# State-space groups of a two-block kernel: a new order of VectorE's and ScalarE's steps, and three VectorE helpers computed head by head

## The reference

```python
def ssd_chunked(x, dt, a, bm, cm, h0, need_y):
    xc = (x * dt[..., None]).reshape(b, nc, SSD_CHUNK, g, r, p)
    cs = jnp.cumsum((dt * a).reshape(b, nc, SSD_CHUNK, g, r), axis=2)
    decay_to_end = jnp.exp(cs[:, :, -1:] - cs)
    chunk_states = jnp.einsum('bclgn,bclgr,bclgrp->bcgrpn', bc, decay_to_end, xc)
    chunk_decay = jnp.exp(cs[:, :, -1])
    def step(hc, inp):
        st, dec = inp
        return hc * dec[..., None, None] + st, hc
    h_last, h_in = lax.scan(step, h0, (chunk_states, chunk_decay))
    lmat = jnp.exp(jnp.where(lower, seg, -jnp.inf))
    cb = jnp.einsum('bclgn,bcsgn->bclsg', cc, bc)
    y = (jnp.einsum('bclsg,bclsgr,bcsgrp->bclgrp', cb, lmat, xc)
         + jnp.einsum('bclgn,bcgrpn,bclgr->bclgrp', cc, h_in, jnp.exp(cs)))
```

## Time and profile before

| | before |
|---|---|
| median of 3 runs | 2844.2 us |
| lowest and highest | 2837.63 and 2851.76 us |
| the profiled execution: its own time | 2849.4 us |
| its span in the trace | 2847.4 us |
| PE busy | 2603.6 us, 91% |
| VectorE busy | 1271.1 us, 45% |
| GpSimd busy | 1637.9 us, 58% |
| ScalarE busy | 913.4 us, 32% |
| mean granted TensorE clock | 0.958 |

### The profile page before, as it was taken

The page is one execution under the profiler, slowest core; times in us unless marked ns, Lnnn a source line. Parts: engine busy times, 40 slices in busy tenths (PEclk is TensorE's granted clock), DMA queues, the critical chain, the costliest instruction groups (busy, mean ns, idle before and its releaser), DMA issues.

```text
span 2847.4 us, 38601 instructions
## 1 busy us (share of the span) xinstructions
PE 2603.6 (91%) x15451; PEld 2224.3 (78%) x15451; DVE 1271.1 (45%) x2224; ACT 913.4 (32%) x1607; POOL 1637.9 (58%) x1414
## 2 busy tenths in 40 slices
PE   6989998999998989989998999989989898879998
PEld 5679987875787777778877788778777777779998
DVE  1545502327646677775123112122454878743311
ACT  2245533115422322224113102042353333243542
POOL 1007775750366666654784788754225676657785
PEclk9999999999899999999999999999989999989999
DMA  6456553237432111112422333332533222245554
GB/s 175 139 166 184 145 133 108 89 122 233 132 98 66 50 47 52 51 38 71 159 89 74 89 102 90 89 104 89 168 124 108 74 63 82 60 126 163 163 155 126
DMA packets 425807, 312.92 MB, mean 110 GB/s; under 512 B 12561, under 2 KB 423219, under 8 KB 424627
## 3 DMA queue, kind: packets, MB, share of 16 engines
q1 hardware_dynamic: 421744, 297.36, 35.4%
q10 hardware_dynamic: 3330, 12.98, 1.2%
q0 software_dynamic: 576, 0.43, 0.2%
HBM read 303.40 MB, written 7.34 MB: 109 GB/s over the span
## 4 chain that ended last, share of the span: by engine, by line
PE 66%; DVE 18%; POOL 7%; issue 5%; ACT 2%; DMA 1%; ACTq 0%; POOLq 0%; DVEq 0%; SPq 0%
PE PS L695 34%; POOL rounded L2506 7%; PE PS L1032 7%; DVE mid_a L2254 5%; PE PS L753 5%; PE PS L718 3%; DVE mid_v L2306 2%; PE PS L1039 2%; PE PS L1159 2%; PE PS L638 2%; PE PS L1081 1%; PE PS L1072 1%; DVE mid_v L2327 1%; PE PS L950 1%; PE PS L962 1%
## 5 line engine op out<-in xcount | busy, mean ns | idle before, releaser
L2506 POOL TENSOR_TENSOR rounded<-ring,rounded 128x512 fp32r<-128x512 f32 (+1 forms) x872 | 1128.3, 1326 | 727.1 <-ACT rounded L1294 487.6
L695 PE MATMUL PS<-rounded 128*128 128x256 f32 (+1 forms) x6864 | 1154.5, 330 | 29.2 <-DVE rounded L2443 8.1
L695 PEld LDWEIGHTS PS<-rounded 128*128 128x128 f32 x6864 | 1026.0, 192 | 154.3 <-issue 23.6
L2529 POOL TENSOR_TENSOR rounded<-ring,constants 128x512 fp32r<-128x512 f32 x216 | 227.4, 1083 | 291.1 <-PE PS L695 148.5
L1032 PE MATMUL PS<-rounded 128*128 128x512 f32 (+1 forms) x1536 | 356.8, 390 | 8.0 <-POOLq L2476 4.4
L1032 PEld LDWEIGHTS PS<-rounded 128*128 128x128 f32 x1536 | 279.7, 191 | 71.1 <-issue 9.1
L1294 ACT ACTIVATE rounded<-ring 128x2048 fp32r<-128x2048 f32 (+1 forms) x99 | 179.8, 1822 | 164.3 <-DMA ring<-in_w_mlp_dram 57.2
L2254 DVE SCALAR_TENSOR_TENSOR mid_a<-PS,V,mid_a 128x510 f32<-128x510 f32 (+3 forms) x256 | 182.0, 713 | 78.2 <-ACT mid_a L1600 71.1
L1039 PE MATMUL PS<-rounded 128*128 128x256 f32 x1152 | 167.8, 309 | 0.0
L1039 PEld LDWEIGHTS PS<-rounded 128*128 128x128 f32 x1152 | 159.6, 213 | 5.9 <-issue 2.4
L2416 DVE SCALAR_TENSOR_TENSOR xT<-PS,mod,xT 128x256 f32<-128x256 f32 x40 | 17.9, 481 | 264.7 <-PE PS L695 264.7
(11 more groups left out here) (244 smaller groups left out, 3288.2 us busy)
## 6 DMA issues: line engine op xcount, KB each, us to landing
ring<-in_w_mlp_dram SPq DMA_DIRECT2D x64, 1024.0 KB, 5.6
ring<-in_w_in_dram SPq DMA_DIRECT2D x56, 1024.0 KB, 5.3
ring<-in_ada_w_dram SPq DMA_DIRECT2D x48, 1024.0 KB, 5.2
ring<-in_w_in_dram SPq DMA_DIRECT2D x81, 512.0 KB, 4.0
ring<-in_w_up_dram SPq DMA_DIRECT2D x44, 512.0 KB, 5.2
ring<-in_w_ssd_o_dram SPq DMA_DIRECT2D x16, 1024.0 KB, 5.7
ring<-in_w_out_dram SPq DMA_DIRECT2D x12, 1024.0 KB, 5.0
ring<-in_w_down_dram SPq DMA_DIRECT2D x16, 704.0 KB, 4.9
```

Of the source, the lines that this page charges most:

```text
L695: mm = pe.matmul(PS[:, b, 0:cols], w[:, k, m * P:(m + 1) * P], x(half * kt + k), start=(half == 0 and k == 0 and n_pass == 0), stop=(half ...
L2506: ins = pool.tensor_tensor(lo[:, r], raw[:, r], hi[:, r], ALU.subtract)
L2529: ins = pool.tensor_tensor(hi[:, r], raw[:, r], ones[:, 0:1].broadcast_to([P, 512]), ALU.mult)
```

## The change

Four things are edited.

1. The order of VectorE's turn: `masks` goes ahead of `taps(0)`; `weights(1)` goes from behind `outputs(0)` to ahead of `starts`; in layer 0 `silu(3)` goes ahead of `outputs(2)`.
2. The order of ScalarE's turn: `tanh_of(0)` goes behind `decays(0)` and `decays(1)`; in layer 0 `tanh_of(2)` goes ahead of the `middle` of tile 3.
3. `weights`, `starts` and `outputs` no longer do one multiplication over all four heads and then one addition. They do one `scalar_tensor_tensor` for each head that does both, with the head's factor as a per-partition scalar. In `weights` that is 4 instructions of 128x128 in place of 2 of 128x512; in each of the two rounds of `starts`, 8 of 128x64 in place of 4 of 128x256; in `outputs`, for each direction, 4 of 128x64 in place of 2 of 128x256. The waits inside (`settle`) that stood between multiplication and addition go.
4. TensorE waits for 8 counts of `hin_ready` in place of 1, since each of the last 8 instructions of `starts` now gives one.

```diff
--- before.py
+++ after.py
@@ -1086,7 +1086,7 @@
 
                     pe.wait_ge(*c.need(m_ready))
                     if t == 0:
-                        pe.wait_ge(*c.need(hin_ready))
+                        pe.wait_ge(*c.need(hin_ready, 2 * GH))
                     else:
                         pe.wait_ge(*c.need(y_done))
                     for r in range(GH):
@@ -1134,7 +1134,7 @@
                 turn_of(0, first=True)
                 counted = [(tile_ready, 4 + nz), (dve_freed, 4 + nz), (chan_ready, 4), (tok_turned, 3),
                            (cb_ready, 1), (seg_in, 2 * ny), (cb_masked, 1), (seg_ready, ny), (tok_ready, 3),
-                           (xw_ready, 6), (st_ready, 1), (m_ready, ny), (hin_ready, 1), (y_done, ny),
+                           (xw_ready, 6), (st_ready, 1), (m_ready, ny), (hin_ready, 2 * GH), (y_done, ny),
                            (y_ready, ny), (split_ready, 4)]
                 counted += [(slot_loaded[(s0 + q) % SLOTS], 32 if q == 2 else 16) for q in range(4)]
                 with c.loop(GROUPS // 2 - 2, [(q, 2 * k) for q, k in counted]):
@@ -1660,9 +1660,9 @@
 
                     after = g + 1 < GROUPS
                     to_tok(first)
-                    tanh_of(1 - p, 0)
                     decays(0)
                     decays(1)
+                    tanh_of(1 - p, 0)
                     if not first:
                         squares_of(last)
                     middle(g, 1 - p, 1)
@@ -1676,10 +1676,12 @@
                     tanh_of(1 - p, 1)
                     if ny > 2:
                         decays(2)
-                    middle(g, 1 - p, 3)
-                    tanh_of(1 - p, 2)
-                    if ny > 2:
+                        tanh_of(1 - p, 2)
+                        middle(g, 1 - p, 3)
                         decays(3)
+                    else:
+                        middle(g, 1 - p, 3)
+                        tanh_of(1 - p, 2)
                     tanh_of(1 - p, 3)
                     if after:
                         round_of_group(g + 1, 2)
@@ -2285,11 +2287,11 @@
 
                 def weights(g, t):
 
-                    lo = dt_lo[:, :, :]
-                    step(dve.tensor_tensor(lo, bc_mid(cb_lo[:, t, :], GH), heads_of(dt, t, 0, g, P), ALU.mult))
                     dve.wait_ge(*c.need(dtu_ready))
-                    settle()
-                    step(dve.tensor_tensor(per_head(dt_up[:, t % 2, :]), lo, per_head(dt_up[:, t % 2, :]), ALU.add))
+                    for r in range(GH):
+                        m = dt_up[:, t % 2, r * P:(r + 1) * P]
+                        step(dve.scalar_tensor_tensor(out=m, in0=cb_lo[:, t, :], scalar=dt[:, t, g * GH + r:g * GH + r + 1], in1=m,
+                                                      op0=ALU.mult, op1=ALU.add))
                     dve.wait_ge(*c.need(e_ready))
                     settle()
                     dve.tensor_tensor(ex[:, t % 2, :], dt_up[:, t % 2, :], PS[:, 7 - t % 2, :], ALU.mult).then_inc(*c.made(m_ready))
@@ -2303,16 +2305,15 @@
                     for n in range(1, 3):
                         settle()
                         for d, order in enumerate((F_STATES, B_STATES)):
-                            step(dve.tensor_tensor(per_head(hin[:, 3 * d + n, :]), per_head(hin[:, 3 * d + n - 1, :]),
-                                                   heads_of(edec, order[n], 128 + 32 * d, g), ALU.mult))
-                        settle()
-                        for d in range(2):
-                            h = hin[:, 3 * d + n, :]
-                            ins = dve.tensor_tensor(h, h, st[3 * d + n], ALU.add)
-                            if n == 2 and d == 1:
-                                ins.then_inc(*c.made(hin_ready))
-                            else:
-                                step(ins)
+                            for r in range(GH):
+                                e, m = 128 + 32 * d + g * GH + r, slice(r * HD, (r + 1) * HD)
+                                ins = dve.scalar_tensor_tensor(out=hin[:, 3 * d + n, m], in0=hin[:, 3 * d + n - 1, m],
+                                                               scalar=edec[:, order[n], e:e + 1], in1=st[3 * d + n][:, m],
+                                                               op0=ALU.mult, op1=ALU.add)
+                                if n == 2:
+                                    ins.then_inc(*c.made(hin_ready))
+                                else:
+                                    step(ins)
 
                 def outputs(g, p, t):
 
@@ -2321,11 +2322,13 @@
                     step(dve.tensor_tensor(ys, PS[:, 3 + t % 2, 0:GW], xd[:, t % 2, :], ALU.add))
                     for d, hs in enumerate((HF, HB)):
                         if t in hs:
-                            step(dve.tensor_tensor(per_head(yi), per_head(PS[:, 5, d * GW:(d + 1) * GW]),
-                                                   heads_of(edec, t, 32 + 64 * d, g), ALU.mult))
                             settle()
-                            step(dve.tensor_tensor(ys, ys, yi, ALU.add))
-                            settle()
+                            for r in range(GH):
+                                e, m = 32 + 64 * d + g * GH + r, slice(r * HD, (r + 1) * HD)
+                                step(dve.scalar_tensor_tensor(out=ys[:, m], in0=PS[:, 5, d * GW + r * HD:d * GW + (r + 1) * HD],
+                                                              scalar=edec[:, t, e:e + 1], in1=ys[:, m],
+                                                              op0=ALU.mult, op1=ALU.add))
+                    settle()
                     dve.scalar_tensor_tensor(out=yg[:, t, bass.ds(g * GW, GW)], in0=ys, scalar=0.5, in1=sz[p][:, t, :],
                                              op0=ALU.mult, op1=ALU.mult).then_inc(*c.made(y_done))
                     settle(y_done)
@@ -2333,17 +2336,17 @@
                 def turn_of(g, p, products=True):
 
                     nxt = g + 1
+                    masks()
                     if products:
                         taps(nxt, 1 - p, 0)
-                    masks()
                     weights(g, 0)
                     if products:
                         silu(1 - p, 0)
+                    weights(g, 1)
                     starts(g)
                     if products:
                         taps(nxt, 1 - p, 1)
                     outputs(g, p, 0)
-                    weights(g, 1)
                     if products:
                         silu(1 - p, 1)
                         taps(nxt, 1 - p, 2)
@@ -2355,9 +2358,10 @@
                         if products:
                             taps(nxt, 1 - p, 3)
                         weights(g, 3)
+                        if products:
+                            silu(1 - p, 3)
                         outputs(g, p, 2)
                         if products:
-                            silu(1 - p, 3)
                             gate_of_z(1 - p, 0)
                         outputs(g, p, 3)
                         if products:
```

## The result

The kernel after runs in 2765.24 us, the median of 4 runs (2760.26 to 2768.98). The kernel before, measured beside it, has 2847.98 us, also over 4 runs (2837.63 to 2852.98). The ratio is 0.9713, with a 95% interval of 0.9679 to 0.9747: faster by 2.9%, against a forecast of 2763 us.

A forecast was written before the change was run, and what follows sets the result against it. TensorE was taken to bound the kernel, held up by a late VectorE. Layer 0's 25 us, layer 1's 47 and its last turn's 9 make 81 us off 2849.4, giving 2768, or 2763 us as median; range 2728 to 2802.

The forecast's parts named there:

- What bounds the kernel: Whole kernel: TensorE, busy 91%; time can be won only where it waits, for a late VectorE, or runs slowly.
- Masks first: Head of each turn: PE's waits for the masks, 1.3 and 1.2 us, go; the delay of `taps(0)` stays hidden.
- Narrow instructions: By-head VectorE instructions: 0.20 us for 64 columns, 0.27 for 128; upper ends 0.28 and 0.35 us.
- the rival of dear narrow instructions: All three helpers: no overlap, 0.28 and 0.35 us per instruction, so 53 us gained, 2791 us; chance 20%.
- `starts`: VectorE ahead of chunk 0: from 6.7 to 4.2 us, since the fused form reads PSUM and runs beside GpSimd.
- Layer 1: Its turns with products: 44.1 us loses 5.0 of waits and 1.7 of slow clock, to 37.4; 47 us over seven.
- the rival "slower": Both layers: `weights` ahead of `starts` holds up TensorE, about 6 us late in layer 1; 2870 us; chance 5%.
- the forecast's own signs of being wrong: `starts` stretched beside GpSimd, a wait for `starts` in layer 1, or a mean layer 0 turn of 61 us or more.
- Layer 0: Its turns: waits 6.6 to 3.1 us (2.1 before chunk 0, 1.0 before chunk 3), slow clock stays; 25 us over seven.
- The clock never falls in layer 0: Rival: the clock holds behind the new 2.1 us wait; 3.3 us more per turn, 23 us, 2740 us; chance 20%.
- The last turn of layer 1: Turn without products: 4.1 us wait goes, of 5.2 some 1.3 stay, about 1 us slow clock goes; 9 us.

The follow-up runs named there:

- the experiment: Kernel after with `masks` put back behind `taps(0)`, nothing else: 2774.01 us, ratio 0.9712 to the kernel before.
- wide `starts`: Kernel after with `starts` alone back as one wide multiplication and one wide addition: 2790.92 us, ratio 0.9781 to the kernel before.
- wide `outputs`: Kernel after with `outputs` alone back as one wide multiplication and one wide addition: 2779.18 us, ratio 0.976 to the kernel before.
- the sum in PSUM: Kernel after with wide `weights`, `silu(3)` behind `outputs(2)`, and the last direction of `outputs` writing its sum to PSUM: 2725.6 us, 0.9555 of before.
- late `silu(3)`: Kernel after with `silu(3)` put back behind `outputs(2)` in layer 0: 2747.96 us, ratio 0.9648 to the kernel before.

## Why the prediction was right

The forecast of 2763 us holds, and its sum of 81 us stands against 82.7 by the medians and 84.6 in the stages touched. The mechanism held; that the total is so near is in part luck, since its parts missed in both directions. By its own steps:

- *What bounds the kernel.* Right: the gain lies in waits of PE for VectorE and in the clock behind them.
- *Masks first.* Right about the wait, gone in both layers. That `taps(0)` behind them costs nothing is right in the steady turns; the experiment shows 5.5 us lost in the first turn of layer 1.
- *Narrow instructions.* 0.20 us from start to start was taken for 64 columns, and (3.28 - 0.28)/15 = 0.20 is measured; 0.28 of length was the upper end, 0.276 to 0.278 is measured. For 128 columns 1.2 us for four, and 1.13 alone. So the rival of dear narrow instructions fell. The Trainium skill's page VectorE: DVE Perf Modes, "Rules for kernel authors", says not to fuse for speed and to minimize the count. Here 320 and 256 narrow instructions in `outputs` and `starts` gained 14 and 26 us (16 and 21 by the turns). The rule is not refuted by that: with GpSimd idle, the wide form took about the same time. The place of an operand outweighed it.
- *`starts`* was to take 4.2 us and takes 4.1 (930.73 to 934.79), untouched by GpSimd. *`weights(0)`* was to take about 4.1 us beside GpSimd and takes 4.25; *`weights(1)`* was put at 3.7 us and takes 2.88. The exclusive lock that the Trainium skill describes in SBUF — State Buffer, "SBUF: two separate sides", fits three readings of the runs: by wide `starts` (2.62 and 0.76 us for the same pair), by wide `outputs` (609 ns) and by the sum in PSUM (833 to 426 ns at the most).
- *Layer 1* is near in its sum and not in its parts. The seven turns went down by 46.7 us, where 47 was said, but 2.9 of that are the wait at the head of the last turn, which the forecast counts there; so it is 43.8. The second to the sixth turn gained 7.7 us each rather than 6.7, down to a PE that never waits, the seventh 5.8 besides that wait, and the first gained nothing (43.9 and 44.2 us). There `dtu` comes late, and `weights(0)` and `weights(1)` take 3.04 and 4.23 us beside GpSimd ahead of `starts`. That is the mechanism of the rival "slower", in one turn of seven, at 5.5 us of wait against the 6 that it named. A wait for `starts` in layer 1 was also one of the forecast's own signs of being wrong, and in that turn it came.
- *Layer 0* is the step that was mis-sized twice. Before chunk 0 the wait was put at 2.1 us with the clock falling; it is 1.0 us with none, since `weights(1)` took 0.8 us less and `weights(0)` began 0.7 us sooner after the masks than the sum had it. So PE came to chunk 3 earlier than in the sum, and waits 2.8 us there, not 1.0; the rest of that miss is the end of `outputs(2)`, 1.36 us beside GpSimd where 0.4 was counted. The trace of before has this length already (1.37 us for L2329 at 966.74, shown with the late `silu(3)`). That makes 3.8 us of wait in all against 3.1, and the two places were swapped. Of the 30.3 us that layer 0 gained, where 25 was said, 19.6 are shorter waits; the sum had 24.5 of them. The other 10.7 are clock, which the sum put at nothing: it was to fall in every turn, and fell in 5 of 7, in two of them for half as long.
- *The clock never falls in layer 0* (20%) came true in 2 of the 7 turns. With `silu(3)` late it is so in six, and about 10 of the 20.3 us gained there are clock. The rival's 23 us is what the clock cost before; in after about half of it was left to gain. Its premise that a wait of 1.4 us shows no fall holds for layer 0 alone (last section).
- *The last turn of layer 1* was to gain 9 us. It gained 6.7, and with the wait at its head, 5.2 to 2.4 us where 1.3 was said to stay, 9.6.

What the forecast did not say is that two parts of the change work against it. `weights` by head costs 12 us and the early `silu(3)` 17: the text saw both prices (four waits for GpSimd in one `weights`, 0.7 to 1 us on the path) and took them into its sum without asking what the change would be worth without them.

## What to carry to other kernels

Before an operation is split or fused on VectorE, look where its two tensor inputs lie: with one in PSUM the pieces of `starts` ran at 0.205 us each beside a busy GpSimd, with both in SBUF those of `weights` each waited out a GpSimd instruction, 1.06 us each in the worst place. So fuse what then reads PSUM, and leave whole what reads SBUF alone. When an edit bundles several moves, price each against the same wait. The gain sat in what came ahead of the end of a wait (`weights(1)`, `starts`); the loss in what was put ahead of it needlessly (`silu(3)`). Shortening that wait from 2.8 to 1.1 us also gave the full clock back.
